# The small inverse of the RWKV-7 mixer: its products on four 32x32 tiles of TensorE instead of two 64x64 tiles

## What is computed

```
def step(S, inp):
    r_t, w_t, k_t, v_t, kk_t, a_t = inp
    sa = jnp.einsum('bhvk,bhk->bhv', S, -kk_t)
    S = (S * w_t[:, :, None, :]
         + sa[..., None] * (kk_t * a_t)[:, :, None, :]
         + v_t[..., None] * k_t[:, :, None, :])
    y = jnp.einsum('bhvk,bhk->bhv', S, r_t)
    return S, y
```

## Time and profile before

| | |
|---|---|
| median of 3 runs | 2967.77 us (2966.18 to 2970.21) |
| profiled execution, first to last instruction | 2963.8 us |
| the median above that span | 4.0 us |
| TensorE matmuls | busy 2899.2 us (98%), 23690 records |
| TensorE weight loads | busy 2474.9 us (84%) |
| VectorE | 1594.7 us (54%) |
| ScalarE | 1000.5 us (34%) |
| GpSimd | 1489.8 us (50%) |
| granted TensorE clock, mean | 0.993 of full speed |

### The profile page before, as it was taken

The page is one execution under the profiler, slowest core; times in us unless marked ns, Lnnn a source line. Parts: engine busy times, 40 slices in busy tenths (PEclk is TensorE's granted clock), DMA queues, the critical chain, the costliest instruction groups (busy, mean ns, idle before and its releaser), DMA issues. The chain is left out here.

```text
span 2963.8 us, 56296 instructions
## 1 busy us (share of the span) xinstructions
PE 2899.2 (98%) x23690; PEld 2474.9 (84%) x23690; DVE 1594.7 (54%) x2059; ACT 1000.5 (34%) x1740; POOL 1489.8 (50%) x1073
## 2 busy tenths in 40 slices
PE   8999999999999999999999999999999999999998
PEld 7888888888888879987888888887998788888887
DVE  7331634267777732329766654544233966664453
ACT  4122211245545432325333332232232533332222
POOL 4554544356666545266554533555427555543254
PEclk9999999989999999999999999999999999999999
DMA  4533455412223231112333356344111233336632
GB/s 160 183 114 96 126 167 183 146 50 61 65 57 80 71 100 43 43 50 76 115 119 140 128 192 223 142 175 156 42 46 49 85 114 135 138 111 238 230 142 85
DMA packets 175988, 346.65 MB, mean 117 GB/s; under 512 B 47233, under 2 KB 104705, under 8 KB 170113
## 3 DMA queue, kind: packets, MB, share of 16 engines
q1 hardware_dynamic: 175744, 343.16, 34.0%
HBM read 240.34 MB, written 102.76 MB: 116 GB/s over the span
## 5 line engine op out<-in xcount | busy, mean ns | idle before, releaser
L820 POOL TENSOR_TENSOR w_lo<-w_raw,w_hi 128x512 fp32r<-128x512 f32 x232 | 333.6, 1462 | 504.5 <-ACT w_hi L1124 501.0
L1679 PE MATMUL ps<-a_hi,w_hi 128*128 128x512 f32 x1140 | 445.3, 391 | 10.4 <-DVE a_lo L2396 10.0
L1679 PE MATMUL ps<-a_lo,w_hi 128*128 128x512 f32 x1140 | 444.3, 390 | 0.0
L1679 PE MATMUL ps<-a_hi,w_lo 128*128 128x512 f32 x1140 | 351.5, 390 | 0.0
L1124 ACT ACTIVATE w_hi<-w_raw 128x512 fp32r<-128x512 f32 x228 | 129.9, 623 | 625.5 <-PE ps L1679 474.7
L2216 PE MATMUL ps<-a_hi,w_hi 128*128 128x512 f32 x800 | 312.4, 391 | 11.5 <-ACT u_t L1499 4.9
L2216 PE MATMUL ps<-a_lo,w_hi 128*128 128x512 f32 x800 | 311.3, 389 | 0.0
L2216 PE MATMUL ps<-a_hi,w_lo 128*128 128x512 f32 x800 | 311.3, 389 | 0.0
L1679 PEld LDWEIGHTS ps<-a_hi,w_hi 128*128 128x128 f32 x1140 | 214.5, 188 | 55.0 <-DVE a_lo L2396 10.0
L1679 PEld LDWEIGHTS ps<-a_hi,w_lo 128*128 128x128 f32 x1140 | 214.3, 188 | 44.8
L1679 PEld LDWEIGHTS ps<-a_lo,w_hi 128*128 128x128 f32 x1140 | 214.5, 188 | 44.2 <-issue 0.2
(11 more groups left out here) (379 smaller groups left out, 6429.3 us busy)
## 6 DMA issues: line engine op xcount, KB each, us to landing
w_raw<-in_weights SPq DMA_DIRECT2D x228, 512.0 KB, 4.1
hidden<-hid SPq DMA_DIRECT2D x44, 1024.0 KB, 3.8
zT<-z_out SPq DMA_DIRECT2D x44, 512.0 KB, 3.3
a_hi<-hidden SPq DMA_DIRECT2D x44, 512.0 KB, 8.3
a_lo<-hidden SPq DMA_DIRECT2D x44, 512.0 KB, 9.4
w_raw<-kvw SPq DMA_DIRECT2D x32, 512.0 KB, 3.3
suv<-zT SPq DMA_DIRECT2D x16, 512.0 KB, 4.7
x<-in_xT SPq DMA_DIRECT2D x16, 512.0 KB, 6.0
```

What stands on the lines that cost most here:

```text
L820: pool.tensor_tensor(low_t[:, part, :], w_raw[:, u, part, :], high[:, part, :].bitcast(F32), ALU.subtract).then_inc(S["w_lo_done"], 1)
L1679: mm = pe.matmul(to[:, nb, 0:w], wt[:, k, :], r[:, k, nb * w:(nb + 1) * w], start=(k == 0 and r is hi_in and wt is high), stop=(k == kn - ...
```

## The change

The products of levels b = 2 to 16 go in 32x32 pieces. At those levels the matrices are block diagonal in 32x32 blocks as far as this level reads them, so of each 64x64 product only the two diagonal 32x32 blocks are made: 32 rows, 32 weight columns, 16 moving columns each. `blocks_of` yields the partitions, the first column and the width; with d innermost the tiles are taken in the order 0, 32, 64, 96 of the diagonal. Level b = 32 gives one piece of 64 as before. The results go to the same places in PSUM, and all waits and increments are as before.

```diff
+            def blocks_of(a, b):
+
+                if 2 * b == C:
+                    return [(lane(a), 0, C)]
+                return [(slice(a * RN + d, a * RN + d + C // 2), d, C // 2) for d in (0, C // 2)]
+
             def cross(n, par, lv):
...
                     for mh, e, a in by_tile():
-                        t_u = inv_t[lane(a), g, 2 * e + mh, :].rearrange("p (n two b) -> p n two b", two=2, b=b)[:, :, 0, :]
-                        mm = pe.matmul(unit(a, g, 2 * L + e * C + mh * 32, 32), atrb[par][lane(a), e, 2 * mh + g, 0, :], t_u,
-                                       start=True, stop=True)
+                        for rows, at, w in blocks_of(a, b):
+                            t_u = inv_t[rows, g, 2 * e + mh, at:at + w].rearrange("p (n two b) -> p n two b", two=2, b=b)[:, :, 0, :]
+                            mm = pe.matmul(ps[rows, g, 2 * L + e * C + mh * 32 + at // 2:2 * L + e * C + mh * 32 + (at + w) // 2],
+                                           atrb[par][rows, e, 2 * mh + g, 0, at:at + w], t_u, start=True, stop=True)
                     mm.then_inc(S["x_ps"], 1)
...
             def merge(n, par, lv):
...
                     for mh, e, a in by_tile():
-                        u_u = inv[par][lane(a), e, 2 * mh + g, :].rearrange("p (n two b) -> p n two b", two=2, b=b)[:, :, 1, :]
-                        mm = pe.matmul(unit(a, g, e * C + mh * 32, 32), xm[lane(a), e, g, mh, :], u_u, start=True, stop=True)
+                        for rows, at, w in blocks_of(a, b):
+                            u_u = inv[par][rows, e, 2 * mh + g, at:at + w].rearrange("p (n two b) -> p n two b", two=2, b=b)[:, :, 1, :]
+                            mm = pe.matmul(ps[rows, g, e * C + mh * 32 + at // 2:e * C + mh * 32 + (at + w) // 2],
+                                           xm[rows, e, g, mh, at:at + w], u_u, start=True, stop=True)
                     mm.then_inc(S["tu_ps"], 1)
```

## The result

The changed kernel takes 3039.06 us (median of 4 runs, 3037.22 to 3042.28). The kernel before, on the same chip, took 2968.9. The ratio is 1.0239, with an interval of 1.0225 to 1.0254: slower by 70 us, where the prediction had 20 us less. The profiled execution has a span of 3036.4 us against 2963.8.

What follows compares the result with a forecast made beforehand. TensorE's in-order list of small products was taken to bound the mixer. 14 groups give 17.5 us, the first and last 1.2 each, 19.9 in all: span 2943.9, plus 4.0 for the median, so 2948 us; range 2935 to 2968.

Steps and rivals of the forecast that it cites:

- Part 1, the phases: In cross and merge 0 to 3, the 64 starts of a phase cover 0.50 us instead of 0.90.
- The rival of a 14 ns floor per start: TensorE's queue starts no load and matmul faster than 14 ns; phases stay at 0.90 us, time 2975; chance 0.12.
- Part 2, changes of shape: Six new changes between 64x64 and 32x32 tiles, around cross and merge 0 and 1, cost 0.10 us each.
- Part 3, one group: Gains and losses through one group in order: 1.29 us shorter, where TensorE alone would have gained 2.3.
- `v_tok` before key_scales: Sign before key_scales: TensorE idle behind ScalarE's `v_tok`, some 0.5 us a group.
- the new state before state_out: Sign after cross 0: TensorE idle before state_out 1 until VectorE ends the new state; no size given.
- the 0.7 ahead of loras: Merge 0, cross 1 and merge 1 get shorter, so loras and ScalarE's tanh come 0.7 us sooner.
- No DMA is added or moved: Closing step of the group's account: the change brings no added or moved transfers; no time counted for any.
- The clock rival: In the mixer the clock falls to its lower level because small tiles count for less work; about 3070 us; chance 0.03.

Runs made afterwards that it cites:

- doubled kernel: Changed kernel with the moving columns of each 32x32 piece streamed twice, the copy into unused PSUM columns: 3019.0 us, ratio 1.0171.
- level 32 in a quarter: Kernel before with level 32's cross and merge products cut to the one 32x32 quarter that matters, same number of instructions: 2966.6 us, ratio 0.9988.

## Why the prediction was wrong

**Part 1, the phases: right.** 64 starts cover 0.55 us at full clock (0.73 less one record of 0.18) where 0.50 was forecast; 8.7 ns a start, 7.7 over the densest 32 starts. The rival of a 14 ns floor per start is refuted.

**Part 2, changes of shape: right.** From the last start of a 64x64 phase to the first of a 32x32 one it is 148 ns, back 121 (medians, doubled kernel; 150 forecast), against some 50 within a shape. The Trainium skill (TensorEngine Tiling (Array Packing), Key Properties) says that a change of tiling mode drains the array, and the trace agrees: each change costs 70 to 100 ns.

**Part 3, one group: right for the sparse part, not for the dense one.** ScalarE's table load starts right behind the copies (810.77 after 810.31 + 0.44), TensorE waits 0.46 us for `v_tok` before key_scales, 11 times in all, and 6 times (2.0 us) for the new state before state_out, as forecast. The sparse part is 14.61 us in a group that doesn't stall, 0.55 less; forecast were 1.29 less the 0.7 ahead of loras, 0.59. Those 0.7 us, in the dense part, never came.

ScalarE after, the chain of the earlier trace rows:

```profile
810.31 0.44 ACT L1206 ACTIVATE xm<-ps 128x128 f32<-128x128 f32 x2
810.77 1.28 ACT L1238 ACT_TABLE_LOAD   x1
...
816.04 0.60 ACT L1264 ACTIVATE v_tok<-ps 128x512 f32<-128x512 f32 x1
```

**The step that failed is "No DMA is added or moved".** The 512 instructions a group were priced by the time that the array needs for them and by nothing else. They come by DMA, 256 a packet. In the mixer of the doubled kernel the packets follow each other every 3.8 us at the median (start to start), the quarter that is closest within 3.6, none closer than 3.3: 256/3.8 = 67 instructions per us, 256/3.6 = 71. The trace of before could have warned: 817 instructions in 12.43 us, 66 per us, and in the mixer 8 issue waits of its own, 4.4 us. The longest of them (before, 633 to 1023 us):

```profile
PE ps L1903 <- issue: 1.5, 1, 1.5
```

256 more at 68 per us are 3.8 us; less some slack, the dense part grew by 3.2 us (12.58 to 15.78 in the doubled kernel) where 0.7 less was forecast. Over 16 groups that is 51 us.

The Trainium skill (Runtime: NRT & Kernel Launch, Instruction fetch mechanics) says that the instructions are refilled in blocks of 16 KiB, 256 instructions each, over a DMA queue of the sequencer, and that this is mostly hidden. The trace agrees on the block (0.52 MB in 32 packets for 8192 instructions) and not on the hiding: some 3 us a group here, and the measurement decides.

**The clock rival, held unlikely, came true as well.** Its reason against ("the engine would be as busy as now") was a reading of the busy column. The granted clock fell (0.85 over the steady mixer) although TensorE was busy 334 of 370 us, and stayed up in the doubled kernel where it was busy for only 313.

**The sum.** From before to the doubled kernel +51 us: the supply, net of what the phases gave back. From there to the kernel after +20: the clock. The two add up to the measured 70 by construction, since each is a difference of times. The five kernels with small pieces in levels 2 and 4 and a clock of 0.986 or more lie at 3007 to 3022; the lowest is the one with 64 instructions fewer.

**What stays open.** That TensorE waits for its instructions is shown by where the waits end. What the time around a packet's transfer is made of, and what asks for the next packet, is not shown, and no run sped the queue up. Of the clock, the pairs above show that the small work moves it, but not why the same small pieces cost 34 us at half clock in the sparse part and 149 in the dense one.

## What to carry to other kernels

Before cutting matmuls into more and smaller ones, count loads and matmuls per us in the densest stretch: near 66 per us, as here, each additional one costs about 15 ns (1/68 us) in that stretch, however little it asks of the array. If there is idle time with no releaser in the middle of a phase, see whether it falls every 256 instructions. Smaller tiles pay where the count stays the same (level 32 in a quarter) and hardly elsewhere. And read the granted clock of each stretch after such a change: TensorE can be busy for 90% of a stretch and still drop to 1.2 GHz.

## What the runs showed of the hardware that was not expected

- TensorE's instruction stream is limited over stretches of several us: in the doubled kernel's dense parts to 68 instructions per us at the median (67 to 73 in single parts; 75 in the fastest part of any kernel), while single runs of 64x64 or 32x32 tiles go at 14.1 and 7.7 ns a matmul, with a load beside each.
- The stream comes in blocks of 256: 456 of 464 issue waits end at the first record of a block, and no block starts sooner than 2.1 us after its packet, whose transfer takes 1.0 us.
- The same instructions with twice the moving columns took 20 us less in all (3019.0 against 3039.1), since the granted clock of the mixer went from 0.85 to 0.99.
- On 32x32 tiles a phase takes nearly as long with 16 moving columns as with 32 (0.55 and 0.56 us for 64 starts), then 0.68 us with 48 and 0.88 with 64: up to 32 the moving columns do not set the pace.
